# A hybrid attention and RWKV-7 encoder layer on one core: the second scan direction's products moved to the other two 64x64 array tiles

## The reference

```python
def step(S, inp):
    r_t, w_t, k_t, v_t, a_t, b_t = inp
    sa = jnp.einsum('zdhij,zdhj->zdhi', S, a_t)
    S = S * w_t[..., None, :] + sa[..., :, None] * b_t[..., None, :] + v_t[..., :, None] * k_t[..., None, :]
    y = jnp.einsum('zdhij,zdhj->zdhi', S, r_t)
    return S, y
```

## Time and profile before

| | |
|---|---|
| median of 3 runs | 2669.78 us (2668.51 to 2673.64) |
| the profiled execution | 2668.92 us, its span 2667.1 us |
| TensorE busy | 2560.4 us, 28304 matmuls |
| DVE, POOL, ACT busy | 1203.4, 817.2, 697.1 us |
| the scan's steps | from 894 to 1545.5 us and a tail to about 1565 |

### The profile page before, as it was taken

How to read it: one execution, slowest core, us unless ns; L and a number is a source line. 1 busy time by engine, 2 the same in 40 slices (tenths; PEclk the granted TensorE clock), 3 DMA queues, 4 the chain that set the end, 5 groups by cost and what they waited for, 6 DMA issues and landing times. The chain is left out here.

```text
span 2667.1 us, 63503 instructions
## 1 busy us (share of the span) xinstructions
PE 2560.4 (96%) x28304; PEld 2143.7 (80%) x28304; DVE 1203.4 (45%) x2312; ACT 697.1 (26%) x1567; POOL 817.2 (31%) x627
## 2 busy tenths in 40 slices
PE   7999999999998799999999979999999999999997
PEld 6785568888887689888888967878888888888885
DVE  3106650001554455555655447554444444444446
ACT  4115651110111344444444333220001100111002
POOL 3322122222331333233232328023233222333234
PEclk9999999999999899999999989999999999999998
DMA  6100011111101000000000025221011111111014
GB/s 161 44 32 17 2 49 72 71 72 72 40 32 50 9 4 4 3 4 4 3 4 4 4 98 203 80 79 40 32 48 40 40 32 37 43 40 40 32 64 142
DMA packets 39084, 123.10 MB, mean 46 GB/s; under 512 B 11424, under 2 KB 11424, under 8 KB 37664
## 3 DMA queue, kind: packets, MB, share of 16 engines
q1 hardware_dynamic: 38816, 119.06, 13.1%
HBM read 96.24 MB, written 20.97 MB: 44 GB/s over the span
## 5 line engine op out<-in xcount | busy, mean ns | idle before, releaser
L1894 DVE TENSOR_TENSOR ff_f<-ff_f,ff_ps 128x512 f32<-128x512 f32 x300 | 205.4, 687 | 173.6 <-PE ff_ps L96 173.6
L1913 DVE TENSOR_TENSOR ff_sq<-ff_rl 128x512 f32<-128x512 f32 (+1 forms) x96 | 128.9, 1342 | 269.2 <-ACT ff_rl L1811 268.6
L1811 ACT ACTIVATE ff_rl<-ff_ps 128x512 f32<-128x512 f32 (+1 forms) x96 | 50.6, 527 | 754.8 <-PE ff_ps L96 754.8
L394 PE MATMUL sc_ps<-sc_xy,sc_q 64*64 64x64 f32 x3200 | 194.7, 219 | 0.0
L1680 POOL TENSOR_TENSOR ff_wd0h<-ff_wdr,params 128x1024 fp32r<-128x1024 f32 x16 | 30.3, 1893 | 460.3 <-DMA ff_wdr<-in_w_down 460.3
L382 PE MATMUL sc_ps<-sc_xy,sc_ai 64*64 64x64 f32 x3200 | 158.0, 221 | 13.0 <-ACT sc_xy L701 6.6
L896 DVE TENSOR_TENSOR sc_q<-sc_ps,sc_cs 128x128 f32<-128x128 f32 x400 | 114.3, 286 | 121.6 <-PE sc_ps L382 120.9
L391 PE MATMUL sc_ps<-sc_q,sc_xy 64*64 64x64 f32 x2560 | 167.2, 220 | 0.0
L253 POOL TENSOR_SCALAR sc_fac<-sc_icl,params,sc_k1a 128x512 f32<-128x512 f32 x20 | 15.4, 768 | 479.5 <-DVE sc_xy L783 417.5
L701 ACT ACTIVATE sc_xy<-sc_ps 128x256 f32<-128x256 f32 x320 | 122.4, 384 | 150.1 <-PE sc_ps L394 149.5
L382 PEld LDWEIGHTS sc_ps<-sc_xy,sc_ai 64*64 64x64 f32 x3200 | 122.7, 134 | 40.1 <-ACT sc_xy L701 30.6
(11 more groups left out here) (300 smaller groups left out, 7281.9 us busy)
## 6 DMA issues: line engine op xcount, KB each, us to landing
ff_wur<-in_w_up SPq DMA_DIRECT2D x32, 512.0 KB, 3.5
ff_wdr<-in_w_down SPq DMA_DIRECT2D x32, 512.0 KB, 4.3
gwr<-in_w_in SPq DMA_DIRECT2D x31, 512.0 KB, 3.2
gm_dram<-gp_gm SPq DMA_DIRECT2D x8, 1280.0 KB, 4.4
ff_m<-gm_dram SPq DMA_DIRECT2D x16, 640.0 KB, 7.7
fr_x<-in_x SPq DMA_DIRECT2D x10, 512.0 KB, 5.6
ff_xs<-in_x SPq DMA_DIRECT2D x10, 512.0 KB, 4.1
x_dram<-ff_xo SPq DMA_DIRECT2D x10, 512.0 KB, 2.9
```

The costliest lines, as they stand in the source:

```text
L394: last = nc.tensor.matmul(y_out[g][rows, u, :], Q1[g][rows, u, :], XY[g][rows, 1, u, :], start=True, stop=True)
L1811: nc.scalar.activation(rl[v % 2][:, 0:tn], ps[:, b, 0:tn], ACT.Relu).then_inc(relu, 1)
L1894: nc.vector.tensor_tensor(own, own, ps[:, 4 + v % 4, :], ALU.add).then_inc(added, 1)
L1913: nc.vector.tensor_tensor(sq[v % 2][:, 0:tn], rl[v % 2][:, 0:tn], rl[v % 2][:, 0:tn], ALU.mult).then_inc(squared, 1)
```

## The change

- For direction u = 1 the products Q (`level_q`), P (`state_in`) and U (`solved`) write to the other head's partitions (`across`), and X (`level_xy`) reads from there and writes back. The operands of these four then lie on the two tiles (rows 0-63, columns 64-127) and (rows 64-127, columns 0-63). Y, the state, the outputs and the preparation stay where they were. X of both directions is now issued ahead of Y of both.
- Y of direction 1 has to lie crossed. `flip` makes it by a matmul of X with the identity, ACT copies it (`flip_copy`); once per group and step. Those of groups 0 to 2 are at the end of the step before, that of group 3 in level 0.
- Two row tiles must not write one bank at once, so each group gets a pair of banks (u = 0 and u = 1), which takes all eight. Gram, token, state, LoRA and side products share banks with the groups (5, 7, 1, 3, 6, 4), so all of them move to the second half of a step, behind a wait for the last level's copies.
- The side products stand in groups 0, 1 and 2 (in block 1: 0 to 3), with waits (`taken`) for DVE's reading; the reciprocal parts move from block 1 and 2 to levels 1 and 3 of blocks 2 and 3; the squares of y to levels 0 to 2 of block 1; the square roots between the copies of P and U.
- The old state is no longer added on TensorE: DVE multiplies it by the decay ahead of time (`keep`) and adds it in the update, now one instruction for each direction.
- `begin` and `turn` of the last group move to the end of the step.

```diff
-GRAM_BANK, TOK_BANK, STATE_BANK, LORA_BANK = 4, 5, 6, 7
+GRAM_BANK, TOK_BANK, STATE_BANK, LORA_BANK = 5, 7, 1, 3
+SIDE_BANK, SPARE_BANK = 6, 4
...
+        pair = [ps[:, 2 * g:2 * g + 2, :].rearrange("p b t -> p (b t)") for g in range(GR)]
+        apart = lambda g, at: ps[:, 2 * g:2 * g + 2, at:at + C]
...
+        other = {0: heads[1], HD: heads[0]}
+        across = lambda rows, u: other[rows.start] if u else rows
...
+            def flip(q, g):
+                n = q * GR + g
+                pe.wait_ge(x1_ready, n + 1)
+                if g == 3:
+                    pe.wait_ge(flipped, n)
+                for rows in heads:
+                    last = nc.tensor.matmul(flip_out[g][across(rows, 1), :], XY[g][rows, X_AT, 1, :], eye[rows, :],
+                                            start=True, stop=True)
+                last.then_inc(flip_ps, 1)
...
                 for u in range(2):
                     for rows in heads:
-                        last = nc.tensor.matmul(q_out[g][rows, u, :], AI[g][rows, u, :], XY[g][rows, 0, u, :],
-                                                start=True, stop=True)
+                        last = nc.tensor.matmul(q_out[g][across(rows, u), u, :], AI[g][rows, u, :],
+                                                XY[g][rows, X_AT, u, :], start=True, stop=True)
...
+                if l < LEVELS - 1:
+                    for u in range(2):
+                        for rows in heads:
+                            at = across(rows, u)
+                            nc.tensor.matmul(x_out[g][rows, u, :], XY[g][at, Y_AT, u, :], Q1[g][at, u, :],
+                                             start=True, stop=True)
                 for u in range(2):
-                    if l < LEVELS - 1:
-                        for rows in heads:
-                            nc.tensor.matmul(x_out[g][rows, u, :], XY[g][rows, 1, u, :], Q1[g][rows, u, :],
-                                             start=True, stop=True)
                     for rows in heads:
-                        last = nc.tensor.matmul(y_out[g][rows, u, :], Q1[g][rows, u, :], XY[g][rows, 1, u, :],
+                        last = nc.tensor.matmul(y_out[g][rows, u, :], Q1[g][rows, u, :], XY[g][rows, Y_AT, u, :],
                                                 start=True, stop=True)
...
             def solved(q, g):
                 n = q * GR + g
-                pe.wait_ge(xy_ready, (q * LEVELS + LEVELS - 1) * GR + g + 1)
                 pe.wait_ge(p_ready, n + 1)
                 for u in range(2):
                     for rows in heads:
-                        last = nc.tensor.matmul(u_out[rows, u, :], XY[g][rows, 1, u, :], PT[g][rows, u, :],
+                        at = across(rows, u)
+                        last = nc.tensor.matmul(u_out[rows, u, :], XY[g][at, Y_AT, u, :], PT[g][at, u, :],
                                                 start=True, stop=True)
...
-                    if not new:
-                        for rows in heads:
-                            nc.tensor.matmul(s_out[rows, u, :], eye[rows, :], S[n % 2][rows, u, :],
-                                             start=True, stop=False)
...
                 for g in range(GR):
                     state_in(q, g)
+                    if g == 0:
+                        side(q, 0)
                     if g == 1:
-                        side_clear(ct, i, 2)
+                        side(q, 2)
+                    if g == 2:
+                        side(q, 4)
+                    if g == 3:
+                        side(q, 5)
...
+            def keep(q, g):
+                i, n = q % NB, q * GR + g
+                if fresh(i, 0, g) and fresh(i, 1, g):
+                    return
+                dve.wait_ge(s_ready, n)
+                nc.vector.tensor_tensor(kept[:, :, :], S[n % 2][:, :, :],
+                                        edge[q % 2][:, g, :].unsqueeze(2).to_broadcast([P, 2, C]),
+                                        ALU.mult).then_inc(kept_ready, 1)
...
+                for u in range(2):
+                    out, by = S[(n + 1) % 2][:, u, :], edge[q % 2][:, g, u:u + 1]
+                    if new[u]:
+                        last = nc.vector.tensor_scalar(out, s_out[:, u, :], by, None, ALU.mult)
+                    else:
+                        last = nc.vector.scalar_tensor_tensor(out, s_out[:, u, :], by, kept[:, u, :],
+                                                              ALU.mult, ALU.add)
+                last.then_inc(s_ready, 1)
```

More of the change, by code:

```diff
@@ new lines, in has_side, with taken, piece_out @@
+            def has_side(ct, i):
+                return ct + 1 < CT if i == 3 else ct > 0
+            def taken(ct, i, n):
+                base = (ct + 1 if i == 3 else ct - 1) * NG
+                pe.wait_ge(done_of[i], base + n)
+            def piece_out(ct, i, p, bank):
+                c = ct - 1
+                if i == 0:
+                    full(bank, mean, y[c % 2], p, mean_ps)
+                if i == 2:
+                    back(bank, norms[1], p, rsb_ps)
+                if i == 3:
+                    back(bank, norms[0], p, rnb_ps)
+                if i == 4:
+                    full(bank, wl[:, c, 4, :], sT[:, E_GL, :], p, gate_ps)
@@ L564, in _ @@
             pe.wait_ge(ta_ready, 2)
+            for g in range(GR):
+                flip(0, g)
             for q in range(STEPS):
-                ct, i = divmod(q, NB)
                 more, ahead = q + 1 < STEPS, q + 2 < STEPS
@@ L577, in _ @@
                     level_q(q, l, 2)
+                    if l == 0 and q:
+                        flip(q, 3)
                     level_xy(q, l, 0)
@@ L603, in _ @@
                     state_out(q, g)
+                    if g == 1:
+                        side(q, 3)
                     outputs(q, g)
-                    if ahead and g == 1:
-                        pe.wait_ge(y_ready, q * GR + 1)
-                        lora_products(q + 2, 1, 0)
                 if more:
                     gram_products(q + 1, GR - 1)
+                    side(q, 6)
+                    if ahead:
+                        pe.wait_ge(ta_ready, q + 3)
+                    for g in range(GR - 1):
+                        flip(q + 1, g)
                     by_token(q + 1, GR - 1)
@@ L734, in _ @@
                 if more:
+                    for g in range(GR - 1):
+                        flip_copy(q + 1, g)
                     token_copy(q + 1, GR - 1)
@@ L925, in _ @@
                         dve.wait_ge(y_ready, ct * NB * GR + far + 1)
-                        nc.vector.tensor_tensor(pair, pair, q_out[g], ALU.add).then_inc(y_ready, 1)
+                        nc.vector.tensor_tensor(pair, pair, o_out[g], ALU.add).then_inc(y_ready, 1)
+                    if g == 0:
+                        side_late(ct, i, 1)
+                    if g == 1 and i != 1:
+                        side_late(ct, i, 2)
+                    if g + 1 < GR:
+                        keep(q, g + 1)
+                    elif more:
+                        keep(q + 1, 0)
                     if ahead and g == 0:
@@ L934, in _ @@
                     mask(q + 1, GR - 1)
+                    begin(q + 1, GR - 1)
+                    turn(q + 1, GR - 1)
             c = CT - 1
```

315 lines of the change are left out of this document (161 added, 154 removed).

## The result

The median went from 2669.78 to 2654.76 us (five runs of each, 2666.85 to 2673.64 and 2646.55 to 2659.10). The ratio is 0.9941, with a 95% interval from 0.9924 to 0.9959. The forecast was 2625 us. So the direction was right and the time lies inside the range, but the gain is 15 us and not 44. The profiled execution took 2659.10 us with a span of 2657.2, so it is the slowest of the five. Compared by spans, the gain in it is 9.9 us.

The account below looks back on a forecast made before the run. TensorE's work and ACT's round trip were taken to bound the levels, DVE the second half; side-product steps -23.1, four without -14, last step -4, block-1 steps -10.8, small losses +7.6, together -44: 2625 us, range 2600 to 2660.

Parts of the forecast that it names:

- the forecast's 0.583: Levels: a group's turn, 0.467 us of array work plus a 0.117 us stall for ACT, making a level 2.33 us.
- The block-1 steps: Four steps whose square-root table load and norms leave the levels; 10.8 us less in all.
- Sum of the levels: 2.2 + 3 x 2.33 + 2.71 = 11.9 us: Levels of one step: level 0, levels 1 to 3 and level 4, against 14.06 us without side products before.
- ACT's round trip: Levels: from a group's last products through ACT's copy to its next Q weight load, 0.700 us over two turns.
- small losses: Reciprocal parts 4.2 us, ACT's squares of K 2.4 and preparation ahead of the scan 1; +7.6 us together.
- work and round trip are in balance here: Levels of the kernel before: TensorE's work, 0.233 + 0.467 us, equals the 0.700 us dependency round through ACT.
- no stretch of the trace sustains: Doubt about four tiles: they want a matmul start every 14.6 ns on average, against 29 ns in the kernel before.
- rival 1: Four-tile products: the issue rate binds, starts stay near 29 ns, levels 2.64 us, gain about 20, 2650 us; chance 10%.
- A step without side products: Four such steps: levels 14.06 to 11.9 us, second half 16.93 to 15.4; given as 3.5 us less each.
- DVE holds the group: Second half: DVE's mask, begin, turn and update set a group's length, 3.5 to 3.6 us against 3.72.
- Rival 3: Crossing products: a change of tile exposes its weight load, some 0.1 us a group, +52 us, 2720 us; chance 8%.

Follow-up runs that it names:

- diagonal again: The changed kernel with only the crossing undone, the second direction's products back on the diagonal tiles: 2675.25 us, ratio 1.0026.
- before, eight waits: The kernel before with eight more waits on a long-fired semaphore ahead of each X/Y block of the levels: 2714.63 us, ratio 1.0166.
- changed, eight waits: The changed kernel with eight extra waits on a long-fired semaphore ahead of every X/Y block of the levels: 2721.15 us, ratio 1.0198.
- changed, fewer instructions: The changed kernel without the second direction's Y product in levels 1 to 3, so the output is wrong: 2616.60 us, ratio 0.9815.
- changed, ACT slower: The changed kernel with one more ACT copy of 16 columns ahead of each copy that releases Q in levels 1 to 3: 2649.31 us, ratio 0.9927.

## Why the prediction was right in kind and wrong in size

**What held.** Four tiles of 64 run together; an 8-instruction group takes 0.117 us (Q's, whose first load waits for ACT, 0.165 to the next block's first matmul). The Trainium skill (TensorE: Matmul & The Clock Gate, "Wait — 56ns, not 53.3ns?") puts start to start at no less than about 25 ns; it does not speak of tiles there. Between different tiles this trace does not agree: starts lie 7 ns apart (1120.036, .042, .049, .056, then .142 and on), 14.6 ns on average. Where no gap falls, the turn is the forecast's 0.583 (level 1, 2.33 to 2.35), with ACT as the releaser. The second halves sum to 371.9 against 376, in part by luck (below). The four groups of (pair 1, block 4) take 4.85, 4.78, 4.62 and 4.60 us, where 5.1, 4.7, 4.6 and 5.0 were given, 18.85 for 19.4. DVE's two-part update takes 0.43, forecast 0.5:

```profile
1147.02 0.43 DVE L860 SCALAR_TENSOR_TENSOR sc_s<-sc_ps,sc_edge,sc_kept 128x64 f32<-128x64 f32 x2
```

The block-1 steps take 35.3, 36.0, 34.9 and 31.2 us against 35.4, 35.4, 34.5 and 30.0, with no clock drop in their levels.

**The step that failed** is "Sum of the levels: 2.2 + 3 x 2.33 + 2.71 = 11.9 us". It gave a level two bounds, the array and ACT's round trip, and took the supply of instructions as free. By sum of the 20 steps, levels 1 to 3 came to 172.5 us and not 140; level 0 to 52.6 and not 44; level 4 to 57.1 and not 54. The gaps are 30.7 us: 27.1 in levels 1 to 3, the rest in level 4, none in level 0. Level 0 has another cause: the flip of group 3 (L393) waits for DVE's turn (L833), 13.0 us in 19 steps, and 4.2 us with the diagonal again, where a level 0 takes 2.35 us. The prediction named this chain and gave it 2.2 us; it takes 2.58. (The 37 us by which the table's levels miss are less than these three together, because the forecast there includes 6.6 us of small losses.) How the supply limits, by kernel: what the levels want where no gap falls, and the gaps of the scan.

| kernel | instructions a turn | turn without a gap, us | so 256 take, us | gaps |
|---|---|---|---|---|
| before | 48 | 0.700 | 3.73 | none |
| diagonal again | 48 | 0.700 | 3.73 | 4, 2.6 us |
| before, eight waits | 52 | 0.758 | 3.73 | 11, 5.1 us |
| changed, eight waits | 52 | 0.74 | 3.64 | 42, 23.8 us |
| changed, fewer instructions | 40 | 0.525 to 0.555 | 3.36 to 3.55 | 19, 10.2 us |
| changed, ACT slower | 48 | 0.61 to 0.65 | 3.25 to 3.47 | 24, 16.4 us |
| changed | 48 | 0.583 to 0.60 | 3.11 to 3.20 | 44, 30.7 us |

Gaps are rare at 3.73 us and common below it. With them, the changed kernel comes back to 3.83 us. This also corrects the sentence "work and round trip are in balance here" about before: a third bound, the supply, stood at nearly the same 0.70 us, and it is the one that did not move. The prediction did weigh that "no stretch of the trace sustains" 14.6 ns a start, and its rival 1 came to 2650, near the time measured. But its mechanism was another: starts did not stay 29 ns apart, whole blocks came late. That its time came near is luck.

**A term that was not in the sum** is the clock. The prediction took the clock drop away from the levels of block 1 and did not ask what the norm's 2-row products do where they now stand, with the crossing beside them. That costs 8.6 to 12.4 us. Without it the second halves are 359.4 us, 17 below the forecast, so in the sum two errors covered each other: side products and group 3 cost less than I gave them (18.34 to 18.85 a half instead of 19.4; 4.60 instead of 5.0), and the clock took most of that back.

**A slip in the sum.** A step without side products was to go from 14.06 + 16.93 to 11.9 + 15.4, which is 3.7 us less and not 3.5; over four steps that is 0.8 us and changes nothing.

**The claim "DVE holds the group"** holds in the kernel before only for group 2, which has no other TensorE work. In groups 1 and 3, with LoRA and the tail, removing L431 was a gain in itself (0.2 us each). In the changed kernel it holds for group 1, which got 0.19 us shorter with the shorter update although TensorE had more to do, and not for groups 2 and 3.

**What stays open.** Why the interval takes just the values 3.47, 3.73 to 3.75 and 4.02 us is not explained. What in the thinner work beside the 2-row products lets the clock fall was not tested by itself. Rival 3, an exposed weight load at a change of tile, did not occur: L427 to L431 goes to the straight tiles in 0.12 us.

## What to carry to other kernels

Before making TensorE's work denser, count its instructions per microsecond (weight load and matmul each, twice for fp32 here) and compare with a stretch of the trace that is known to run without "issue" gaps; here some 256 in 3.7 us was the most that lasted. A stall that nothing releases, at a fixed count of instructions, is supply, and only fewer instructions help, not a faster engine or a shorter wait. When small-contraction matmuls are moved out of a dense stretch, or the work beside them is thinned, look at the granted clock behind them; here more rows against zeros cost no time and kept it up.

## What the runs showed of the hardware

- Four 64x64 tiles in fp32 overlap fully: 8 instructions of 64 columns in 0.117 us, with the two row tiles of a column half writing banks of their own.
- Instructions are fetched in packets of 16.4 KB, 256 instructions, and dense fp32 products of 64 columns outrun them: gaps of 0.25 to 1.3 us, 128 weight loads apart, or 118 when 4 of 52 instructions are waits. Packets are fetched one at a time; from a gap's end over the next packet (0.88 to 1.44 us) to the next gap's end it is 3.47 to 4.02 us.
- A wait that is long fulfilled is not free on TensorE. Eight of them (4 instructions) lengthened a turn from 0.700 to 0.758 us in before. In the last level, where the group's own chain binds, they cost 0.2 us a group (3.17 to 4.05 for four).
- Four of the five stretches at half clock lie in halves of a step with matmuls of 2 contraction rows; with 32 rows the scan's half-clock time fell from 34.1 to 3.3 us at the same duration of the products. With 2 rows but the second direction's products back on the diagonal it was 4.4 us.
